# Two VectorE steps moved, one swap, and paired stores in a two-block model kernel

## The reference, cut to what matters

```
first_block:                       # after an rmsnorm and x @ w_in (3592 columns)
  o_a = rmsnorm(hgrn2(silu(q), k, v, log_f)) * silu(g_a)     # 4 heads of 64, gated recurrence
  o_b = pooled means (windows 2/4/8/16) @ pool_w * silu(g_b) # 4 groups of 64
  o_c = forgetting attention, 8 heads of 64  * silu(g_c)
  x   = x + rmsnorm(concat(o_a, o_b, o_c) @ w_out)
second_block:
  out_a = windowed attention with ALiBi and sinks; out_b = latent attention with rope (SC96 = 96 ** -0.5)
  x = x + rmsnorm((sigmoid(g_a) * (out_a @ w_o_a) + sigmoid(g_b) * (out_b @ w_o_b)) @ w_out)
  x = x + rmsnorm(square(relu(rmsnorm(x) @ w_up)) @ w_down)  # d_ff = 4096
```

## Time and profile before

| | |
|---|---|
| median of 3 runs | 955.13 us |
| the profiled execution | 955.45 us |
| its span | 954.2 us |
| TensorE busy | 946.1 us, 99% |
| VectorE, ScalarE, GpSimd busy | 586.5, 417.8, 96.5 us |
| chain that ended last | PE 90%, DVE 6%, ACT 2%, issue 1% |
| DMA | 85.99 MB, 90 GB/s in the mean |
| granted TensorE clock | 1.0 over the profiled execution |

### The profile page before, as it was taken

How to read it: one execution, slowest core, us unless ns; L and a number is a source line. 1 busy time by engine, 2 the same in 40 slices (tenths; PEclk the granted TensorE clock), 3 DMA queues, 4 the chain that set the end, 5 groups by cost and what they waited for, 6 DMA issues and landing times.

```text
span 954.2 us, 13502 instructions
## 1 busy us (share of the span) xinstructions
PE 946.1 (99%) x5250; PEld 777.6 (82%) x5250; DVE 586.5 (61%) x1062; ACT 417.8 (44%) x773; POOL 96.5 (10%) x106
## 2 busy tenths in 40 slices
PE   9999999999999999999999999999999999999998
PEld 8779777777898777777778889988888888888897
DVE  6668759797658787765666725863244344445545
ACT  6455346455645456544553234562342233212322
POOL 2004204320220000000002312000000000000021
PEclk9999999999999999999999999999999999999999
DMA  6321122122324111111222352443233322322102
GB/s 245 98 80 67 46 67 67 46 67 78 111 72 184 71 60 60 64 60 46 89 67 89 113 175 69 137 172 112 90 107 93 107 89 89 110 90 93 40 1 89
DMA packets 25806, 85.99 MB, mean 90 GB/s; under 512 B 2960, under 2 KB 5968, under 8 KB 25488
## 3 DMA queue, kind: packets, MB, share of 16 engines
q1 hardware_dynamic: 24384, 79.92, 25.6%
q10 hardware_dynamic: 1120, 4.88, 1.4%
q0 software_dynamic: 240, 0.33, 0.2%
HBM read 80.93 MB, written 4.19 MB: 89 GB/s over the span
## 4 chain that ended last, share of the span: by engine, by line
PE 90%; DVE 6%; ACT 2%; issue 1%; DMA 0%; DVEq 0%; ACTq 0%
PE PB L411 13%; PE PB L413 13%; PE PB L412 13%; PE PB L993 5%; PE PB L995 5%; PE PB L994 5%; PE PB L633 4%; PE PB L670 3%; PE PB L648 2%; PE PB L696 2%; PE PB L873 2%; PE PB L874 2%; PE PB L456 2%; PE PB L875 2%; PE PB L451 1%; PE PB L452 1%
## 5 line engine op out<-in xcount | busy, mean ns | idle before, releaser
L411 PE MATMUL PB<-hh,wh 128*128 128x512 f32 x576 | 235.2, 408 | 0.0
L413 PE MATMUL PB<-hh,wl 128*128 128x512 f32 x576 | 224.9, 390 | 0.0
L412 PE MATMUL PB<-hl,wh 128*128 128x512 f32 x576 | 224.6, 390 | 0.0
L1487 DVE TENSOR_TENSOR wl<-raw,wh 128x1024 fp32r<-128x1024 f32 (+2 forms) x90 | 113.2, 1258 | 53.1 <-ACT wh L1033 53.0
L411 PEld LDWEIGHTS PB<-hh,wh 128*128 128x128 f32 x576 | 108.1, 188 | 28.2 <-issue 6.4
L412 PEld LDWEIGHTS PB<-hl,wh 128*128 128x128 f32 x576 | 108.3, 188 | 23.1 <-issue 2.2
L413 PEld LDWEIGHTS PB<-hh,wl 128*128 128x128 f32 x576 | 108.1, 188 | 23.3
L1033 ACT ACTIVATE wh<-raw 128x1024 fp32r<-128x1024 f32 (+2 forms) x90 | 91.3, 1019 | 55.0 <-PE PB L875 12.7
L1196 ACT ACTIVATE S<-S,sm 128x256 f32<-128x256 f32 (+3 forms) x96 | 50.7, 529 | 106.1 <-DVE sm L1590 80.8
L1487 DVE TENSOR_TENSOR wl<-AR,wh 128x1024 fp32r<-128x1024 f32 x55 | 67.6, 1230 | 40.4 <-ACT wh L1033 40.4
L1033 ACT ACTIVATE wh<-AR 128x1024 fp32r<-128x1024 f32 x55 | 57.9, 1052 | 71.0 <-PE PB L995 71.0
(11 more groups left out here) (374 smaller groups left out, 1691.3 us busy)
## 6 DMA issues: line engine op xcount, KB each, us to landing
AR<-in_dne SPq DMA_DIRECT2D x32, 512.0 KB, 3.5
AR<-in_upe SPq DMA_DIRECT2D x24, 512.0 KB, 3.5
raw<-in_w2g SPq DMA_DIRECT2D x16, 512.0 KB, 3.4
raw<-in_w1e SPq DMA_DIRECT2D x10, 512.0 KB, 3.4
raw<-in_w1q SPq DMA_DIRECT2D x8, 512.0 KB, 3.4
raw<-in_woab SPq DMA_DIRECT2D x8, 512.0 KB, 3.5
raw<-in_w2e SPq DMA_DIRECT2D x5, 512.0 KB, 5.0
X<-in_xT SPq DMA_DIRECT2D x4, 512.0 KB, 6.7
```

The lines of the kernel that those rows point to most:

```text
L411: e.matmul(bank[:], a[:, col(k)], xa[:, k, :], start=k == 0, stop=False)
L412: e.matmul(bank[:], a[:, col(k)], xb[:, k, :], start=False, stop=False)
L413: i = e.matmul(bank[:], b[:, col(k)], xa[:, k, :], start=False, stop=k == 7)
L1487: e.tensor_tensor(low_, raw_of(c), high.bitcast(F32), ALU.subtract).then_inc(*up("lo", c))
```

## The change

It has four parts. The head norm of pair 0 on VectorE moves from beat REC[0] + 29 to REC[0] + 33. The low part of the chunk that is due after w1e 9 comes behind the gates' code of that beat instead of ahead of it. `rotated_first` is called ahead of the low parts and gates of its beat. All four stores of the first half are issued by SyncE, and tiles 0 to 5 of the second half are stored in three transfers of two tiles, with tile 6 ahead of the third.

```diff
-NORMED = [REC[0] + 29, REC[1] + 18]
+NORMED = [REC[0] + 33, REC[1] + 18]
...
+        def store_two(e, i):
+
+            t = half_of[1]
+            e.wait_ge(*to(*result_tile(2 * i + 1)))
+            e.dma_start(out.rearrange("(k p) t -> p k t", p=128)[:, 2 * i:2 * i + 2, t],
+                        X[:, 2 * i:2 * i + 2, t]).then_inc(semaphore(f"out{i}c"), 16)
...
             root_half(3, 1)
-            for i in (1, 3):
-                store(e, i, 0)
             for k in BY_PE:
...
                 for c, end in END1.items():
-                    if t == end + 1:
+                    if t == end + 1 and c < CH["w1e", 9]:
                         lo(c + 2)
...
                         e.tensor_tensor(o, o, z, ALU.mult).then_inc(*up("silu", s, p))
+
+                if t == END1[CH["w1e", 9]] + 1:
+                    lo(CH["w1e", 9] + 2)
...
+                if t == PAIRS + 1:
+                    for m in range(2):
+                        rotated_first(m)
                 for c, beat_of in LOW2.items():
                     if t == beat_of:
                         lo(c)
...
                 if t == PAIRS + 1:
-                    for m in range(2):
-                        rotated_first(m)
                     for m in range(2):
                         rotated(m)
...
-            for i in (0, 2):
+            for i in range(4):
                 store(e, i, 0)
-            for k in (0, 1, 2, 3, 6, 4, 5):
-                store(e, k, 1)
+            store_two(e, 0)
+            store_two(e, 1)
+            store(e, 6, 1)
+            store_two(e, 2)
             for i in range(4):
                 e.wait_ge(semaphore(f"out{i}a"), 16)
-            for k in range(8):
+            for i in range(3):
+                e.wait_ge(semaphore(f"out{i}c"), 16)
+            for k in (6, 7):
                 e.wait_ge(semaphore(f"out{k}b"), 16)
```

## The result

The changed kernel took 957.09 us (median of 20 executions, 955.62 to 957.65), the kernel before 955.22 (20, 954.97 to 955.49): ratio 1.0015, with an interval from 1.0009 to 1.0021. The prediction said 955.6 and a range up to 956.6, so it was wrong: 1.87 us slower, not 0.5.

What follows compares the result with a forecast made beforehand. TensorE, busy 946.1 of 954.2 us at full clock, was taken as the bound. Terms -0.69 + 2.20 - 0.80 + 0 - 0.20 = +0.51 on 955.13 gave 955.6 us; the 8-in-10 range was 953.5 to 956.6.

Steps and rivals of the forecast that it cites:

- the term +2.20 in part 1: Root's four instructions at beat 42 delay the keys' copy, so TensorE stands 2.20 us before the states (L716, later L723).
- Part 1, removed: Root gone from beat 38: VectorE empties banks 6 and 7 sooner, TensorE's wait at L696 goes, -0.69 us.
- So nothing more: Behind L716 the state copies still come before L728, so VectorE's lag of 0.65 us costs TensorE nothing further.
- Part 2: At the last gate (beat 56), L1753 empties the bank before the low part; TensorE's wait at L451 goes, -0.80 us.
- Part 3: Moving rotated_first leaves VectorE's instruction order and the wait of L648 unchanged: 0, bounds 0 and -0.5 us.
- Part 4: Stores at the kernel's end: last pair issued 0.6 us earlier, -0.20 us taken, bounds -0.45 and +0.3.
- The bound from the bytes: Final stores: eight 131 KB halves at 344 GB/s need 3.05 us, ending at 953.85, no earlier than before: 0.
- Rival A: At beat 42 the four instructions cost nothing, VectorE being ahead or L716 not needing the keys: -1.69, 953.4 us; chance 0.15.
- Rival C: Moving rotated_first does reorder VectorE's instructions, beats being miscounted by one: 0.5 us less, 955.1; chance 0.08.
- Rival B: Beats 43 to 46: late VectorE work collides with GpSimd's pool sums, lag grows, 1 to 1.5 us, 956.6 to 957.1; chance 0.13.
- The 0.2% from no change: Whole kernel: a measurement can tell about 0.2%, 1.9 us, from no change; below 953.2 faster, above 957.0 slower.
- The chance of 0.07 for slower: Whole kernel: chance 0.07 of a time above 957.0 us, needing the VectorE collision with GpSimd at its upper end.

Runs made afterwards that it cites:

- the second measurement: The changed kernel measured once more with nothing altered: 955.87 us (11 executions), ratio 1.0014.
- the kernel with the root alone: The kernel before with only the head-norm root of pair 0 moved to beat 42: 956.97 us, ratio 1.0024.
- the kernel with all four at beat 45: The changed kernel with the four VectorE instructions of pair 0's head-norm root and gain at beat 45 instead of 42: 957.61 us, ratio 1.0022.

## Why the prediction was wrong

The step that failed is the price of the term +2.20 in part 1. The mechanism is as written: the keys' copy is late, L723 stands 2.25, and no wait on the way takes it up. But the prediction took a stand of TensorE to cost its own length. It had read that the granted clock was 1.0 in all slices and put the clock behind a stand at nothing, without a reason. In 21 of 41 executions the clock falls behind that stand, for a further 1.58. In two of the three measurements, the one on record among them, the median lay above the lower group for that. Which group the median falls in is chance: with the median of the second measurement, 955.87, the same kernel would have stood near the forecast, and the missing price would not have been seen.

The Trainium skill, in "TensorE: Matmul & The Clock Gate", section "HAM oscillation — how this bites in real kernels", says that stretches in which TensorE waits bring the clock down, and that work run at the low level takes twice as long. The traces agree in kind: 0.43 against 0.23 a multiplication. In length they differ from the page: the waits in its example are of 3 to 5 us and lose the clock every time, while here a single one of 2.2 us lost it in 21 of 41 executions, and the measurement decides.

Point by point:

- Part 1, removed: predicted -0.69, measured -0.69. 
- Part 1, added: predicted +2.20, measured +2.25, plus 1.58 in half of the executions. VectorE was indeed not ahead at beat 42: what it gained at 176 is given up in its wait for L640, 2.3 long where it was 0.4, and its wait L1765 for ScalarE is still 1.6, followed by the four instructions. But "So nothing more" was wrong: VectorE's lag does not die out behind L723, and it is the 0.24 more at the last gate in the kernel with the root alone.
- Part 2: predicted and measured -0.80 (-0.87 by medians alone). The margin was thinner than the sum had it: L1758 ends at 232.82, 0.11 ahead of TensorE's L458, where the sum had 0.39 (231.65 less 231.26), because of that same lag.
- Part 3: predicted and found to be no reordering. The -0.5 of its bound was not there to be had: the real reordering that was tried gives nothing.
- Part 4: predicted -0.20, measured -0.09 in the trace and 0 to 0.2 between medians. The last pair was issued when the prediction said, 0.6 earlier than before once the 0.36 by which TensorE is late there is taken off. Tile 7 took 2.46 to land where it took 2.06, right behind the last pair. The bound from the bytes (eight halves at 344 GB/s end no earlier, 953.85) was the better guide than the times of issue: the last landing is at 954.26, less 0.36 that is 953.90.
- Rival A, absorbed: false, the wait of L723 is there. Rival C: false, the order is that of the earlier trace rows.
- Rival B had the right side and the right size (956.6 to 957.1) by the wrong mechanism. Of VectorE's work beside GpSimd's sums one instruction grew, L1577 from 1.02 to 1.31, and no wait of TensorE followed from it; the low part is 2.33 after and before, in this row of the trace after:

```profile
209.89 2.33 DVE L1492 TENSOR_TENSOR wl<-raw,wh 128x1024 fp32r<-128x1024 f32 x1
```

- The 0.2% from no change: +0.20% by the medians (1.0015 by the ratio), on the edge of what was called the same (up to 957.0). The chance of 0.07 for slower was too low, as what a new stand brings beside its length can only cost time.

What stays open: why one execution keeps the clock behind the same 2.2 us and the next does not; and, as no profile of the changed kernel fell in its upper group, the place of the low stretch in that kernel itself.

## What to carry to other kernels

When a change makes the bounding engine stand somewhere for two microseconds, price the stand, and beside it price the clock behind it: here 1.6 us in half of the executions. If the times of a kernel widen, list them one by one and set each beside its mean granted clock before a median is believed; then fill the stand with harmless multiplications, which tells the clock from a late input in one run. Better than either is to put the moved work into a wait that its own engine already has: that kernel took 953.85, 0.3 less than with the root in its old place and 1.9 less than the lower group of the changed one. The work has to stand inside the wait. Ahead of the instruction that starts what is waited for, it only moves the wait along, as at 225 in the kernel with all four at beat 45.

## What the runs showed of the hardware

- The granted clock fell to 1.2 GHz behind a single stand of 2.2 us in the middle of 950 us of otherwise dense work, in 4 to 5 of 10 executions, behind 3.55 us in all five and behind 1.4 us in none of 11. Low stretches lasted 3.4 us in both profiles that hold one; one began 0.2 us before TensorE started again, the other 0.7 us after.
- With the stand of 2.2 us filled by nine multiplications of ones, no execution of 11 lost the clock.
- A 128 KB store issued 0.28 behind a 256 KB one of another engine took 2.46 to land, against 2.06 behind stores of its own size (2.46 to 2.47 and 2.06 to 2.08 in the other traces).
